# A decoder block with a mixture of experts on one core: the last expert block taken out of the loop, its rows added by one-hot products

## The reference

```python
def reference(x, ...):                       # x: 1 x 512 x 1024, float32, one layer
    xn = rms_norm(h, norm_mix_g)
    proj = xn @ w_in
    o_att = moba_attention(q, k, v, slopes)  # 8 heads of 64
    o_rwkv = rwkv7_time_mix(...)             # 8 heads of 64
    h = h + concatenate([o_att * attn_norm_g, o_rwkv]) @ w_out
    xn2 = rms_norm(h, norm_ffn_g)
    h = h + moe_ffn(xn2, ...)                # top 4 of 32 experts for each token
    return rms_norm(h, norm_final_g)
# moe_ffn, for each expert e and the tokens t routed to it:
#   gate = minimum(xn2[t] @ w_gate[e] + b_gate[e], 7)
#   up   = clip(xn2[t] @ w_up[e] + b_up[e], -7, 7)
#   y[t] += g[t, e] * (((up + 1) * gate * sigmoid(1.702 * gate)) @ w_down[e] + b_down[e])
```

## Time and profile before

| what | us |
|---|---|
| median of 3 runs | 1593.2 |
| lowest and highest run | 1591.2, 1597.9 |
| span of the profiled execution | 1595.7 |
| TensorE busy in it | 1526.1 (96%) |
| VectorE busy | 1326.0 (83%) |
| ScalarE busy | 1082.8 (68%) |
| GpSimd busy | 628.6 (39%) |

### The profile page before, as it was taken

How to read it: one execution, slowest core, us unless ns; L and a number is a source line. 1 busy time by engine, 2 the same in 40 slices (tenths; PEclk the granted TensorE clock), 3 DMA queues, 4 the chain that set the end, 5 groups by cost and what they waited for, 6 DMA issues and landing times.

```text
span 1595.7 us, 29403 instructions
## 1 busy us (share of the span) xinstructions
PE 1526.1 (96%) x10445; PEld 1262.4 (79%) x10445; DVE 1326.0 (83%) x1458; ACT 1082.8 (68%) x1309; POOL 628.6 (39%) x366
## 2 busy tenths in 40 slices
PE   7999987889999999999999999999999999999993
PEld 6877777876888888888888888888888888888872
DVE  4256555544699999999999999999999999999994
ACT  4245531103478888788888888888878888878881
POOL 7000312101032234345545545545555555665532
PEclk9999999998999999999999999999999999999996
DMA  8321110001499999999999999999999999999974
GB/s 291 94 67 40 40 41 3 3 4 67 172 344 397 385 394 373 394 367 396 384 379 394 389 395 392 389 368 391 386 395 392 385 380 382 397 391 390 381 289 129
DMA packets 81414, 464.81 MB, mean 291 GB/s; under 512 B 11658, under 2 KB 12870, under 8 KB 33216
## 3 DMA queue, kind: packets, MB, share of 16 engines
q1 hardware_dynamic: 71424, 438.68, 69.6%
q0 software_dynamic: 9248, 25.05, 7.1%
q10 hardware_dynamic: 672, 0.07, 0.0%
HBM read 449.16 MB, written 23.66 MB: 296 GB/s over the span
## 4 chain that ended last, share of the span: by engine, by line
PE 85%; DVE 9%; issue 2%; DMA 2%; ACT 1%; POOL 0%; DVEq 0%; POOLq 0%; ACTq 0%; SPq 0%
PE banks L376 70%; PE banks L1799 5%; DVE expert_w_lo L316 5%; PE banks L2062 1%; PE banks L2059 1%; PE banks L1892 1%; PE banks L1876 1%; PE banks L1997 1%; PE banks L2044 1%; DMA gate_bias_rows<-in_moe_b_gate_dram 1%; PE banks L1919 0%; PE banks L2071 0%; PE banks L2322 0%; PE banks L2299 0%; DMA y_sums<-y_block,scatter_rows 0%
## 5 line engine op out<-in xcount | busy, mean ns | idle before, releaser
L316 DVE TENSOR_TENSOR expert_w_lo<-expert_w_raw,expert_w_hi 128x1024 fp32r<-128x1024 f32 x764 | 907.7, 1252 | 25.5 <-ACT expert_w_hi L311 24.9
L311 ACT ACTIVATE expert_w_hi<-expert_w_raw 128x1024 fp32r<-128x1024 f32 x764 | 746.4, 1056 | 17.3 <-DMA expert_w_raw<-in_moe_w_down_dram 15.0
L376 PE MATMUL banks<-expert_w_hi,x_block_T_hi 128*128 128x512 f32 x992 | 389.2, 392 | 1.3 <-DVE expert_w_lo L316 1.3
L376 PE MATMUL banks<-expert_w_lo,x_block_T_hi 128*128 128x512 f32 x992 | 386.5, 390 | 0.0
L376 PE MATMUL banks<-expert_w_hi,x_block_T_lo 128*128 128x512 f32 x992 | 386.4, 390 | 0.0
L726 POOL COPY scatter_gates<-slot_gate 128x1 f32 x26 | 240.3, 9244 | 239.6 <-DMA y_sums<-y_block,scatter_rows 239.6
L376 PE MATMUL banks<-expert_w_hi,h_block_T_hi 128*128 128x512 f32 x544 | 216.0, 397 | 5.3 <-DVE h_block_T_lo L1189 3.4
L376 PEld LDWEIGHTS banks<-expert_w_hi,x_block_T_hi 128*128 128x128 f32 x992 | 186.4, 188 | 40.5 <-issue 1.7
L376 PEld LDWEIGHTS banks<-expert_w_lo,x_block_T_hi 128*128 128x128 f32 x992 | 186.3, 188 | 39.0
L376 PEld LDWEIGHTS banks<-expert_w_hi,x_block_T_lo 128*128 128x128 f32 x992 | 186.4, 188 | 37.7
L376 PE MATMUL banks<-expert_w_lo,h_block_T_hi 128*128 128x512 f32 x544 | 212.9, 391 | 0.0
(11 more groups left out here) (382 smaller groups left out, 1965.2 us busy)
## 6 DMA issues: line engine op xcount, KB each, us to landing
expert_w_raw<-in_moe_w_up_dram SPq DMA_DIRECT2D x128, 1024.0 KB, 6.4
expert_w_raw<-in_moe_w_down_dram SPq DMA_DIRECT2D x128, 1024.0 KB, 9.0
expert_w_raw<-in_moe_w_gate_dram SPq DMA_DIRECT2D x126, 1024.0 KB, 9.0
w_raw<-in_w_in_dram SPq DMA_DIRECT2D x24, 512.0 KB, 4.0
residual<-in_x_dram SPq DMA_DIRECT2D x8, 512.0 KB, 5.1
w_raw<-in_w_out_dram SPq DMA_DIRECT2D x8, 512.0 KB, 3.6
y_sums<-v_shifted SPq DMA_DIRECT2D x5, 512.0 KB, 7.9
staged_raw<-in_moe_w_gate_dram SPq DMA_DIRECT2D x2, 1024.0 KB, 5.9
```

What stands on the lines that cost most here:

```text
L311: act.activation(self.hi[:, k % self.nhl, 0:width], self.raw[:, slot, 0:width], ACT.Copy)\
L316: dve.tensor_tensor(self.lo[:, k % self.nhl, 0:width], self.raw[:, (k - self.staged) % self.nraw, 0:width], self.hi[:, k % self.nhl, 0:wid ...
L376: last = pe.matmul(o, lhs, rhs, start=start and t == 0, stop=stop and t == 2, skip_group_check=preset)
```

## The change

Block 31 is no longer an iteration of the loops of TensorE, VectorE and ScalarE; it is written out behind them (`block_pe(last_blk, True)` and its likes), with these differences:

- The transposes of the next x block are left out. After chunk 3 of block 30's down projection TensorE transposes h of block 31 and the table of gates instead; h goes into `xbh` and `xbl`, which are free by then. ScalarE's split and its copy of the table stand where the split of x stood.
- The last down projection goes into banks 0 and 1, chunks 0 to 3 first, then half 0 of chunks 4 to 7, then half 1.
- Its rows aren't scattered. ScalarE and VectorE evict them, scaled, as high and low part (`y_hi`, `y_lo`, in the space of `hbh`, `hbl`). GpSimd makes a matrix `ohT` (slot by token, one where the slot belongs to the token). TensorE starts each tile's PSUM banks with the bias product and adds `ohT` times `y_hi` and `y_lo`.
- `sum_d` starts as the residual: SP stores each tile of `H` there (`store_sums`) beside the stores of `xn2`, and only the spare rows are zeroed at the start. GpSimd waits for these stores ahead of its first gather.
- SP loads `sum_d` back into `H` when the scatter-add of block 30 has landed. VectorE adds the PSUM banks by halves, ScalarE squares by halves, GpSimd adds the two sums ahead of its two operations, and the scaling of a tile stands two tiles behind its adds.
- `y_may_go` of block 31 no longer waits for the landing of the scatter-add before.

Left out of the diff are the new tiles' allocations (they follow all others) and a renamed wait in `evict`.

```diff
--- before
+++ after
...
+
+y_hi, y_lo = (b[:, :, :].rearrange("p k t -> p (k t)") for b in (hbh, hbl))
+
+def last_bank(tt):
+
+    return pair[(1, 2, 3, 0)[tt]]
...
-    for tt in range(TT + 1):
-        sp.dma_start(sum_d[tt * P:(tt + 1) * P, :], VX[:, 0:2, :].rearrange("p a t -> p (a t)"))\
-            .then_inc(S("sums_zeroed"), 16)
+    sp.dma_start(sum_d[TT * P:(TT + 1) * P, :], VX[:, 0:2, :].rearrange("p a t -> p (a t)"))\
+        .then_inc(S("spare_zeroed"), 16)
...
+    def store_sums(tt):
+        sp.wait_ge(S("mix_added"), 2 * tt + 2)
+        sp.dma_start(sum_d[tt * P:(tt + 1) * P, :], H[:, tt, :]).then_inc(S("rows_stored"), 16)
+
...
+        store_sums(tt)
...
+    store_sums(3)
...
-    last_blk = sp.value_load(n_blk[0:1, 1:2], min_val=NE - 1, max_val=NB - 2)
+    last_blk = sp.value_load(n_blk[0:1, 1:2], min_val=NE - 4, max_val=NB - 5) + 3
...
-    sp.wait_ge(S("y_stored"), nb * 16)
+    sp.wait_ge(S("rows_stored"), 16 * TT)
+    sp.wait_ge(S("y_stored"), last_blk * 16)
...
-        sp.dma_start(raw2[:, tt, :], sum_d[tt * P:(tt + 1) * P, :]).then_inc(S(f"sums_in_{tt}"), 16)
+        sp.dma_start(H[:, tt, :], sum_d[tt * P:(tt + 1) * P, :]).then_inc(S(f"sums_in_{tt}"), 16)
...
-            sp.dma_start(out[0, tt * P:(tt + 1) * P, fs], H[:, tt, fs]).then_inc(S("out_stored"), 16)
-    sp.wait_ge(S("out_stored"), 32 * TT)
+            sp.dma_start(out[0, tt * P:(tt + 1) * P, fs], H[:, tt, fs]).then_inc(S("rows_stored"), 16)
+    sp.wait_ge(S("rows_stored"), 48 * TT)
...
+    pool.iota(iotaT[:, :], [[1, SEQ]], base=0, channel_multiplier=0, allow_small_or_imprecise_dtypes=True)
...
+    pool.wait_ge(S("spare_zeroed"), 16)
+    pool.wait_ge(S("rows_stored"), 16 * TT)
...
-    scatter(last_blk - 1, at, last_blk)
+    ic.base, ic.n = at + ch.n, 0
+    ic.link(pool.tensor_copy(last_row[:, :], idx_y[:, ds(last_blk, 1)]))
+    pool.sem_inc(S("index_ready"), 1)
+    pool.tensor_scalar(ohT[:, :], iotaT[:, :], last_row[:, 0:1], None, ALU.is_equal).then_inc(S("rows_ok"), 1)
+    scatter(last_blk - 1, at + 1, last_blk)
+    y_may_go(last_blk, at + 2)
+    pool.tensor_tensor(pow_ready[:, :], onesf[:, 0:1], neghalf[:, :], ALU.pow)
...
-    y_may_go(last_blk, at + 1)
-    scatter(last_blk, at + 2, nb)
-    pool.tensor_tensor(pow_ready[:, :], onesf[:, 0:1], neghalf[:, :], ALU.pow)
-    pool.wait_ge(S("y_stored"), nb * 16)
...
+        tc.link(pool.tensor_tensor(v, half_ss[:, 2 * tt:2 * tt + 1], half_ss[:, 2 * tt + 1:2 * tt + 2], ALU.add))
...
-def block_act(act, i):
+def block_act(act, i, final=False):
...
-    xT_hi(act, i + 1)
+    if final:
+        split_hi(act, xbh, (S("hT_ps"), i + 1), S("hT_hi"))
+        act.wait_ge(S("gmapT_ps"), 1)
+        act.activation(gmapT[:, :], bank[2][:, 0:P], ACT.Copy).then_inc(S("gmapT_ok"), 1)
+    else:
+        xT_hi(act, i + 1)
...
-    with act.Fori(0, NE - 3) as it:
+    with act.Fori(0, NE - 4) as it:
...
-            i = it + NE
-            with act.If(i < nb):
+            i = it + (NE - 1)
+            with act.If(i < last_blk):
...
+    block_act(act, last_blk, True)
...
-    hT_hi(act, last_blk)
-    act.wait_ge(S("gmapT_ps"), 1)
-    act.activation(gmapT[:, :], bank[0][:, 0:P], ACT.Copy).then_inc(S("gmapT_ok"), 1)
...
-    y_act(act, base_of(nb) + 8, nb)
+    act.wait_ge(S("y_free"), nb)
+    for f in range(2):
+        act.wait_ge(w_used, base_of(nb) + (5 + f))
+        act.activation(y_hi[:, 512 * f:512 * f + 512], bank[f], ACT.Copy, scale=now_g[:, 0:1])\
+            .then_inc(hi_done, 1)
...
-        act.wait_ge(S("combined"), tt + 1)
-        act.activation(pair[tt][:, :], H[:, tt, :], ACT.Square,
-                       accum_out=ss[:, 8 + tt:9 + tt]).then_inc(S("squares_ok"), 1)
+        for f in range(2):
+            act.wait_ge(S("combined"), 2 * tt + f + 1)
+            ins = act.activation((HB, UP, SG, BG)[tt][:, 512 * f:512 * f + 512], H[:, tt, 512 * f:512 * f + 512], ACT.Square,
+                                 accum_out=half_ss[:, 2 * tt + f:2 * tt + f + 1])
+        ins.then_inc(S("squares_ok"), 1)
...
-def block_dve(dve, i, over_part=None):
+def block_dve(dve, i, over_part=None, final=False):
...
-    xT_lo(dve, i + 1)
+    if final:
+        split_lo(dve, xbl, xbh, (S("hT_hi"), i + 1), S("hT_ok"))
+    else:
+        xT_lo(dve, i + 1)
...
-            dve.tensor_scalar(n_blk[:, 1:2], bend[:, NE - 1:NE], -1.0, None, ALU.add)
+            dve.tensor_scalar(n_blk[:, 1:2], bend[:, NE - 1:NE], -4.0, None, ALU.add)
...
-    with dve.Fori(0, NE - LOOP0) as it:
+    with dve.Fori(0, NE - LOOP0 - 1) as it:
...
-            i = it + NE
-            with dve.If(i < nb):
+            i = it + (NE - 1)
+            with dve.If(i < last_blk):
...
-    for k in range(5):
+    block_dve(dve, last_blk, None, True)
+    for k in range(8):
...
-    hT_lo(dve, last_blk)
-    for k in range(5, 8):
-        xring.make_lo(dve, base_of(nb) + k, UP0 + k)
+    for f in range(2):
+        dve.wait_ge(hi_done, base_of(nb) + (9 + f))
+        fs = slice(512 * f, 512 * f + 512)
+        dve.scalar_tensor_tensor(y_lo[:, fs], bank[f], now_g[:, 0:1], y_hi[:, fs].bitcast(F32),
+                                 ALU.mult, ALU.subtract).then_inc(lo_done, 1)
+    dve.wait_ge(S("late_params_in"), 16 * 5)
+
+    def scaled_out(tt, f):
+        hs = H[:, tt, 512 * f:512 * f + 512]
+        dve.wait_ge(S("rms_ok"), 2 * TT + tt + 1)
+        dve.scalar_tensor_tensor(hs, hs, rms[:, 8 + tt:9 + tt], g_fin[:, 512 * f:512 * f + 512],
+                                 ALU.mult, ALU.mult).then_inc(S("final_ok"), 1)
...
-        dve.wait_ge(S("down_bias_ps"), tt + 1)
-        ins = dve.tensor_tensor(H[:, tt, :], H[:, tt, :], pair[(0, 1, 3, 2)[tt]][:, :], ALU.add)
-    ch.link(ins)
-    dve.wait_ge(S("y_stored"), nb * 16)
-    for tt in range(TT + 1):
-        if tt < TT:
-            dve.wait_ge(S(f"sums_in_{tt}"), 16)
-            dve.tensor_tensor(H[:, tt, :], H[:, tt, :], raw2[:, tt, :], ALU.add).then_inc(S("combined"), 1)
-        if tt >= 1:
-            t = tt - 1
-            dve.wait_ge(S("rms_ok"), 2 * TT + t + 1)
-            dve.wait_ge(S("late_params_in"), 16 * 5)
-            for f in range(2):
-                hs = H[:, t, 512 * f:512 * f + 512]
-                dve.scalar_tensor_tensor(hs, hs, rms[:, 8 + t:9 + t], g_fin[:, 512 * f:512 * f + 512],
-                                         ALU.mult, ALU.mult).then_inc(S("final_ok"), 1)
+        dve.wait_ge(S(f"sums_in_{tt}"), 16)
+        for f in range(2):
+            hs = H[:, tt, 512 * f:512 * f + 512]
+            dve.wait_ge(S("last_sum_ps"), 2 * tt + f + 1)
+            dve.tensor_tensor(hs, hs, last_bank(tt)[:, 512 * f:512 * f + 512], ALU.add)\
+                .then_inc(S("combined"), 1)
+        if tt >= 2:
+            scaled_out(tt - 2, 0)
+            scaled_out(tt - 2, 1)
+    for tt in (TT - 2, TT - 1):
+        for f in range(2):
+            scaled_out(tt, f)
...
-    def block_pe(i):
+    def block_pe(i, final=False):
...
-            if c == 1:
+            if final and c == 3:
+                pe.wait_ge(S("h_ok"), i + 1)
+                block_transpose(HB[:, :], S("hT_ps"))
+                flip(bank[2][:, 0:P], gmap[:, :]).then_inc(S("gmapT_ps"), 1)
+            if c == 1 and not final:
...
-    with pe.Fori(0, NE - LOOP0) as it:
+    with pe.Fori(0, NE - LOOP0 - 1) as it:
...
-            i = it + NE
-            with pe.If(i < nb):
+            i = it + (NE - 1)
+            with pe.If(i < last_blk):
...
-    pe.wait_ge(S("xT_ok"), nb + 2)
-    pe.wait_ge(S("h_ok"), nb)
-    block_transpose(HB[:, :], S("hT_ps"))
+    block_pe(last_blk, True)
+
+    def last_down(c, f):
+        n, k = base_of(nb) + c, UP0 + c
+        fs = slice(512 * f, 512 * f + 512)
+        pe.wait_ge(lo_done, n + 1)
+        last = three(pe, bank[f], whi2[:, k % NHL2, fs], wlo2[:, k % NHL2, fs], xbh[:, c, :], xbl[:, c, :],
+                     c == 0, c == KT - 1, True)
+        if (c < 4 and f == 1) or c == KT - 1:
+            last.then_inc(w_used, 1)
+
+    def down_bias(tt):
+        rows = slice(32 * tt, 32 * tt + 32)
+        for f in range(2):
+            pe.matmul(last_bank(tt)[:, 512 * f:512 * f + 512], gmapT[rows, :], bd4[rows, 512 * f:512 * f + 512],
+                      start=True, stop=False, skip_group_check=True)
+
+    def last_sum(tt, f):
+        fs = slice(512 * f, 512 * f + 512)
+        pe.wait_ge(lo_done, base_of(nb) + (9 + f))
+        for y in (y_hi, y_lo):
+            last = pe.matmul(last_bank(tt)[:, fs], ohT[:, tt * P:(tt + 1) * P], y[:, fs],
+                             start=False, stop=y is y_lo, skip_group_check=True)
+        last.then_inc(S("last_sum_ps"), 1)
+
...
-    flip(bank[0][:, 0:P], gmap[:, :]).then_inc(S("gmapT_ps"), 1)
-    pe.wait_ge(S("y_act"), last_blk)
...
-    for c in range(8):
-        chunk(base_of(nb) + c, UP0 + c, pair[2], hbh, hbl, c, c == 0)
-    pe.wait_ge(S("up_ok"), nb)
+    for c in range(4):
+        for f in range(2):
+            last_down(c, f)
+    for f in range(2):
```

(20 more changed lines are left out.)

14 lines of the change are left out of this document (9 added, 5 removed).

## The result

The changed kernel runs in 1580.3 us (median of 7 runs, 1575.2 to 1588.1), the kernel before in 1593.2 us beside it (7 runs, 1590.6 to 1597.9). The ratio is 0.9921 with a 95% interval of 0.9901 to 0.9942. In a later comparison the same kernel gave 0.9898 (0.9868 to 0.9928). The forecast was 1579.5.

What follows compares the result with a forecast made beforehand. The prediction took TensorE to bound the loop, with gains only at the end: 14.0 us off the tail, head 0, less 0.3 for peeling, leaves 13.7; 1593.2 - 13.7 = 1579.5 us, range 1575.5 to 1586.5.

Steps and rivals of the forecast that it cites:

- Transposes and stalls: Block 30's down projection: early transposes of h bring TensorE stalls of 0.65 and 1.0 us; the projection ends 1.8 us later.
- The last down projection: Block 31, by halves: 11.2 us at full clock, its end moving from 1567.05 to 1562.7, 4.3 us gained.
- 2.8 us earlier: Start of the last down projection: at once after block 30's, instead of at 1554.27.
- The clock: TensorE around the last down projection: drop taken as 0, bounded by 1.9 us; rival 1581 to 1584, chance 0.10.
- Scatter-add of block 30: Tail: issued at 1554.1, landing 7.7 us later at 1561.8, with 1560.3 and 1568.5 as ends; loads follow.
- the rival: Tail: block 30's scatter-add takes 11.4 to 14.4 us and becomes the bound, 1583 to 1586; chance 0.14.
- TensorE and the loads meet within half a microsecond: First add in the tail: sums loaded at 1565.4, first product in at 1565.8, so the end hangs on both.
- GpSimd: Tail: one-hot matrix fits VectorE's pause (1542.1 to 1546.5); gate copy held until 1559.3, just in time for the 1560.0 eviction.
- From the first add to the end: Tail: from 1565.8, VectorE's adds and scalings end at 1577.2, then 4.5 us of stores and rest, end 1581.7.
- Peeling at 0.3: Ahead of block 31: loop exit, load of two counts and untaken branch now fall there, costing 0.3 us.
- The head at 0, bounds -0.5 and +3: Start of the kernel: four residual stores of 512 KB ahead of block 1's gather cost 0 us, bounds -0.5 and +3.
- Only the scatter-add saved: Tail rival: new order costs what the early start gives, only scatter-add and load less products saved: 6.8 us, 1586.4; chance 0.08.

Runs made afterwards that it cites:

- after_again: The changed kernel run once more, unaltered, for a second profile: tail 61.8 us, against 61.9 in its first profile.
- late_flip: Changed kernel with the transposes of h of block 31 and their splits back behind block 30's down projection: tail 62.1 us, ratio to before 0.9909.
- splits_behind: Changed kernel with the last high and low parts of block 30's down projection put ahead of the splits of h: tail 59.35 us, ratio to before 0.9877.
- last_scattered: Changed kernel with block 31's rows evicted whole and scatter-added, no one-hot sums: tail 74.7 us, ratio to before 0.9977.
- short_tail: splits_behind with GpSimd's configuration change called for earlier and the third tile's bias products moved behind the first one-hot products: tail 61.1 us, ratio to before 0.9904.
- no_scatter30: Changed kernel without block 30's scatter-add, the sums loaded once block 29's has landed: tail 62.0 us.
- neither: Changed kernel without block 30's scatter-add and without the bias products of the down projection: tail 61.0 us.
- before_rows_stored: Kernel before plus four 512 KB stores of the residual at the head, GpSimd's first gather waiting for them: head 115.4 us, ratio to before 1.0004.

## Why the prediction was right, and where its steps were not

The total is right: 13.7 us were forecast, 12.9 and 13.8 measured by medians. It is that close in part by luck. The sum was one for the tail, with the head at 0, and the tail gained 14.7 us in the profiles: 1.0 us more than forecast, which the head takes back in some runs. Step by step, with times counted from the mark (the prediction's own, less 1519.1):

- **Transposes and stalls.** Forecast at 24.2, found at 24.05. Two stalls of 0.65 and 1.0 us were forecast, the brackets show 0.69 and 0.66 (and 1.21 for the second in after_again). The eighth low part was late by 0.17, forecast 0.35. Block 30's eviction starts at 32.9, forecast 33.1. This step held.
- **The last down projection.** Its end was to move to 43.6; its last matmul starts at 43.8 in after, 47.6 in before. 3.8 us gained, not 4.3, at the full clock. Right in kind, 0.5 us too large: this term of the sum was mis-sized.
- **What that step is worth against another order** is where the working misled. I booked "2.8 us earlier" as a merit of the early transposes. late_flip gets 3.4 of the 3.8 us with the transposes in their old place: 1.05 because the unused transposes of a next x block are gone (block 31's stand at 29.5 and not at 30.55), 0.7 by the shorter wait, and 1.7 by the clock that didn't fall in its one profile. And splits_behind shows that 2.5 us lay in the order that I took as given; I had computed its stalls from ScalarE's queue, and they came, but not asked what they cost against the queue the other way round.
- **The clock.** I took 0, with the drop tied to a wait of 3.4 us. The 0 is borne out: no drop in the tail of after and after_again, nor in the six others with the same transposes, behind waits of up to 1.21 us. That the length of the wait decides is not: in this tail there were drops behind 3.40, 3.44 and 3.64 us and none behind 2.69, but the head has drops behind 2.08 and 2.09, and the mixer both behind 2.73.
- **Scatter-add of block 30.** Issue at 34.9, forecast 35.0; landing after 7.40 us, forecast 7.7. last_scattered shows that it can be 11.4, where the rival began (11.4 to 14.4).
- **"TensorE and the loads meet within half a microsecond."** The first add came at 46.9, forecast 46.7, released by TensorE. Its two sources were 1.15 us apart, not half: the load landed at 45.6 (forecast 46.3), the product at 46.8 (46.7). They do meet at the fifth add, where the third load, landed at 49.5, binds by 0.1 us. Inside, two errors cancel: the down projection ended 0.6 us later than forecast, and three tiles of bias took 2.00 and not 2.44 us. The 2.44 came from dividing a row that has a wait in it (short_tail above). The fourth tile took 1.98 and not 0.8, hidden behind VectorE's adds.
- **GpSimd.** Wrong twice, with no price. The one-hot matrix was to fit in VectorE's pause; GpSimd needed 8.30 us of "issue" first and made it at 1554.4 (30.0 behind the mark). The scatter-add was not held up, by luck: the matrix and the copy behind it were done 0.4 us before ScalarE's eviction, which was late as forecast. The gate copy was to be held until the end of VectorE's run; it took 1.21 us in the middle of it. The Trainium skill (GPSIMD Engine Reference, 1. Specifications) has VectorE's instructions with two SBUF inputs contend with GpSimd. The copy of 1535.03 agrees: it took 8.72 us and ended with VectorE's run of thirteen low parts. That of 1561.45 does not: 1.21 us beside the same instructions, and in no_scatter30 and neither it took 0.25. What tells them apart is open.
- **From the first add to the end.** VectorE's last ends at 57.8, forecast 58.1, though the first add was 0.2 us later than forecast; the end 4.1 us later, forecast 4.5. From the first add to the end that is 0.9 us less than forecast.
- **Peeling at 0.3.** No run shows this cost: TensorE has no pause at the transposes of after, nor between block 30's down projection and the last.
- **The head at 0, bounds -0.5 and +3.** The stores cost nothing (before_rows_stored). The spread inside the bounds lies in waits for low parts; why they differ from run to run is open.
- **The rivals.** Block 30's scatter-add is not the bound (no_scatter30: no gain). The clock did not fall. "Only the scatter-add saved" would have been a tail of 69.8; it is 61.9. TensorE has no wait at the transposes of block 1, so the gather was in time.

## What to carry to other kernels

When the work that ends a chain is moved to other engines, ask what its resource was holding up beside: here a scatter-add also kept the gate copy and with it the next eviction, so that one late landing cost 2.9 us in last_scattered. And look at the waits before giving a part its share: taking the one-hot sum out cost 12.7 us in its one profile, but some 10 without that late landing. Before booking a gain as a merit of a new order, price the nearest other orders: one changed range of two loops gave 2.5 us on top of the change. And price small groups of instructions by the rows of a group of that size, not by dividing a larger one.

## What I had not expected of the hardware

- GpSimd stands 8.1 to 10.5 us in front of its one-hot comparison in the nine profiles in which two MODIFY_POOL_CONFIG instructions belong to it (8.30 in after, 9.21 in late_flip, 10.39 and 10.54 in no_scatter30 and neither); in before they belong to the power, and the pause of 8.59 us is there. If a power operation comes first, that one has 11.43 us of "issue" ahead of it and takes 8.02 itself, beside VectorE's run, and the comparison then follows its cast after 0.23 us. Such an operation is best put where GpSimd has nothing due.
- In the tail TensorE's clock fell to the lower level (1.2 GHz, 0.43 us a matmul) behind waits of 3.40, 3.44 and 3.64 us and stayed at the upper one (2.4 GHz, 0.23 us) behind 2.69 us and behind a wait filled with other matmuls. A fall cost 1.4 to 2.4 us. Elsewhere in the same traces it fell behind 2.08 us, and behind the same 2.73 us in some profiles and not in others, so one profile does not show that a wait is safe.
- Products with 32 rows on different quarters of the array run side by side: one, two and three tiles of four instructions all take 2.0 us.
- Block 30's scatter-add of 512 KB, with no weights under way, landed after 6.4 to 7.5 us in eleven profiles and after 11.41 in one, so a single row of it is a weak base for a sum.
